# Two FFNs of an fp32 block: weight splits one unit further ahead, five plain pairs instead of six in the first

## The chip, the cores and the metric

The kernel runs on one core of a Trainium2 chip. The metric is the device time in microseconds (us) of one execution; 0.2% of it is 3.6 us.

## The reference, cut to what matters

One sequence of 512 tokens with 1024 features goes through an FFN, a mixer (short convolution and gated linear attention), a second FFN, and then a second block (neighbourhood attention, retention, a squared-ReLU MLP). All of it is float32. The change concerns the two FFNs, which are alike:

```python
def rmsnorm(x, g):
    xf = x.astype(jnp.float32)
    y = xf * lax.rsqrt(jnp.mean(xf * xf, axis=-1, keepdims=True) + EPS)
    return (y * g.astype(jnp.float32)).astype(x.dtype)

def swiglu(x, w_gu, w_down):          # w_gu: 1024 x 5632, w_down: 2816 x 1024
    g, u = jnp.split(x @ w_gu, 2, axis=-1)
    return (jax.nn.silu(g) * u) @ w_down

x = x + 0.5 * swiglu(rmsnorm(x, norm_ffn1_g[l]), ffn1_w_gu[l], ffn1_w_down[l])
x = x + hybrid_mixer(...)
x = x + 0.5 * swiglu(rmsnorm(x, norm_ffn2_g[l]), ffn2_w_gu[l], ffn2_w_down[l])
```

## The kernel before, in words

Activations lie transposed in SBUF: 8 tiles of 128 features x 512 tokens. TensorE multiplies in fp32r, so each fp32 operand is kept as a rounded high part and a low part that holds the rest, and a product is three matmuls: high x high, high x low, low x high.

**Units.** The whole program is a list of units (`_units`, line 81), numbered from 0, in the order in which TensorE takes them. A plain unit is one column tile of a weight matrix, 128 output features: 8 blocks x 3 matmuls of 512 columns (`unit`, line 1870; matmuls on L1884 to L1886). The weights of a unit are loaded by SyncE into `raw`, rounded by ScalarE into `wh` (`hi`, L526) and split by VectorE into `wl` (`lo`, L1065), which TensorE waits for. `raw`, `wh` and `wl` are rings of three plain units: ScalarE can round the weights of a unit only when TensorE is through with the unit three before it (`WF`, line 525).

**Pairs.** An FFN has 22 gate/up pairs (in groups of 8, 8 and 6, `FG`) and after each group 8 down units (`w_d`). The first `JS[f]` pairs of FFN f are plain: a gate unit and an up unit, 48 matmuls of 512 columns. The others are factored pairs (`pair`, line 1939): the 2x2 blocks of the two units are computed by seven products in place of eight, 7 x 4 x 3 = 84 matmuls of 256 columns. They need other operands:

- sums of weight blocks: `total` (VectorE, L1088), each then rounded (`pair_hi`, L536) and split (`pair_lo`, L1072) in half units of 512 columns;
- sums of activation blocks, built once per FFN for four values of `kp` by three steps on VectorE and one on ScalarE: `normed` (L1114, two instructions, needs the norm factor R), `sums_of_blocks` (four on L1119 to L1124), `operands` (ScalarE rounds them into BThi, L561), `low_blocks` (VectorE, the low part BTlo, L1128). TensorE starts the first factored pair when the fourth `low_blocks` is done (line 1944).

Between the products of a pair ScalarE copies partial results out of PSUM (`tap`, L552), and the third product waits for the first such copy (line 1950).

**What a plain pair j does on VectorE** (`ffn`, line 1202): the gate half times R (`times_r`, L1192), `low_blocks` of the previous pair's operands, silu times R (L1208), the product with the up half (L1249), the splits of two coming weight units, one step of the operands, and the low part of the result (`a_lo`, L1200). ScalarE does the silu (L588), two roundings, the high part of the result (L615) and `operands`.

**The order** is written out by hand for each engine, in two loops that mirror one another (`ffn` of ScalarE at line 585 and of VectorE at line 1202); each engine works through its own list in order. In the first FFN the norm factor is known only when units 0 to 2 are through: `norm` (line 577 and line 1168) takes one table load and three instructions on ScalarE (L571 to L575) between VectorE's L1160 and L1164. With `JS = (6, 5)` the first FFN has six plain pairs (units 0 to 11), and the operands are built from its third pair on (`normed(0, 0)` at the end of the second); the second FFN has five, and builds from its first.

Of the kernel before, what the change touches and what calls it, by code (L numbers as in the profile page):

```python
# [7 lines left out]
ALU = mybir.AluOpType  # L8
# [11 lines left out]
FT = FF // P  # L20
# [37 lines left out]
        self.eng.wait_ge(self.sem, self.n)  # L58


JS = (6, 5)
NP = 7

UNITS = []
# [214 lines left out]
def build(nc, dr, out):  # L279
# [20 lines left out]
    R, _ = sb("R", [P, T])  # L300
    SS, _ = sb("SS", [P, T])
    SS2, _ = sb("SS2", [P, T])
# [109 lines left out]
    def layer(u):  # L412
        return (u >= U0["ffn2"]) + (u >= U0["mlp"])

    def sums_of(p):
        return SS[:, :], SS2[:, :], TA[8], (TA[6], TA[7], SW3[:, :])[layer(p)]

    def part(p, c):

# [96 lines left out]
    def act_program(act):  # L516
# [60 lines left out]
        def norm(c):  # L577
            act.preload_act_table_set(LN_SET)
            rows(c, TA[6], TA[7], TA[8])
# [5 lines left out]
        def ffn(f, after):  # L585
# [8 lines left out]
            for g, (a, b) in enumerate(FG):  # L594
                for j in range(a, min(b, JS[f])):
                    u = GU[f, g] + 2 * (j - a)
                    if f == 0 and j == 0:
                        hi(3)
                        hi(4)
                        norm(1)  # L600
                    elif f == 0 and j == 1:
                        hi(5)
                    elif not JS[f] - 5 < j:
                        feed(u + 2)
                    if f == 1 and j == 0:
                        norm(6)
                    silu(u, j)
                    if f == 0 and j == 1:
                        hi(6)
                    elif f == 1 or j > 1:  # L610
                        feed(u + 3)
                    if f == 0 and j == 2:
                        operands(0, 0)
                    act.wait_ge(s["ev"], EVN[u + 1])
                    act.activation(Ahi[:, j - a, :], TA[6 + j % 2], ACT.Copy).then_inc(s["ah"], 1)  # L615
                    if JS[f] - 5 <= j < JS[f] - 1 and (f == 1 or j > 1):
                        feed(u + 4)
                        operands(f, j - JS[f] + 5)
                first = max(a, JS[f])
                for j in range(first, b):  # L620
                    p, v = GU[f, g] + 2 * (j - a), GU[f, g] + 2 * (j - a) + 2
# [428 lines left out]
    def dve_program(dve):  # L1050
# [114 lines left out]
            own.wait()  # L1165
            return lambda dst: dve.scalar_tensor_tensor(out=dst, in0=m, scalar=1.5, in1=y, op0=ALU.add, op1=ALU.mult)

        def norm(c, r):
            mean(c, TA[6], D)
            newton(c, TA[6], TA[7], TA[8])(R[:, :]).then_inc(s["r"], 1)  # L1170
            dve.wait_ge(s["r"], r)

# [27 lines left out]
            dve.tensor_tensor(Alo[:, j, :], src, f32(Ahi[:, j, :]), ALU.subtract).then_inc(s["al"], 1)  # L1200

        def ffn(f, after, sums):
            def gate(u, j):
                times_r(u, TA[j % 2])
                if JS[f] - 5 < j and (f == 1 or j > 2):
                    low_blocks(f, j - JS[f] + 4)
                dve.wait_ge(s["silu"], f * FT + j + 1)
                own.add(dve.tensor_tensor(TA[4 + j % 2], TA[2 + j % 2], R[:, :], ALU.mult))  # L1208

            def product(p, j):  # L1210
                dve.wait_ge(s["silu"], f * FT + j + 1)
                dve.wait_ge(s["ev"], EV0[p] + 2)
# [5 lines left out]
            for g, (a, b) in enumerate(FG):  # L1218
                for j in range(a, min(b, JS[f])):
                    u = GU[f, g] + 2 * (j - a)  # L1220
                    if f == 0 and j == 0:
                        lo(3)
                        lo(4)
                        norm(1, 1)
                    elif f == 0 and j == 1:
                        lo(5)
                    elif f == 0 and j == 2:
                        sums_of_blocks(0, 0)
                    elif j == JS[f] - 1:
                        total(u + 2, 0)  # L1230
                        total(u + 2, 1)
                        pair_lo(u + 2, 0)
                        pair_lo(u + 2, 1)
                    else:
                        feed(u + 2)
                    if f == 1 and j == 0:
                        norm(6, 3)
                    gate(u, j)
                    if f == 0 and j == 1:
                        lo(6)  # L1240
                    elif j < JS[f] - 1 and (f == 1 or j > 1):
                        feed(u + 3)
                    if f == 0 and j == 2:
                        low_blocks(0, 0)
                    if JS[f] - 5 <= j < JS[f] - 1 and (f == 1 or j > 1):
                        normed(f, j - JS[f] + 5)
                    dve.wait_ge(s["pe"], PEN[u + 1])
                    own.wait()
                    dve.tensor_tensor(TA[6 + j % 2], BK[BANK[u + 1]][:, :], TA[4 + j % 2],  # L1249
                                      ALU.mult).then_inc(s["ev"], 1)  # L1250
                    if f == 0 and j == 1:
                        normed(0, 0)
                    if JS[f] - 5 <= j < JS[f] - 1 and (f == 1 or j > 1):
                        sums_of_blocks(f, j - JS[f] + 5)
                    if j == JS[f] - 1:
                        pair_lo(u + 2, 2)
                        total(u + 2, 2)
                        pair_lo(u + 2, 3)
                    dve.wait_ge(s["ev"], EVN[u + 1])
                    a_lo(38 * f + a, j - a, TA[6 + j % 2])  # L1260
                    if j == JS[f] - 1:
                        total(u + 2, 3)
# [1269 lines left out]
```

## Time and profile before

| | |
|---|---|
| median of 3 runs | 1792.57 us (1792.3 to 1792.79) |
| profiled execution, its own time | 1793.07 us |
| its span | 1791.4 us |
| TensorE busy | 1780.2 us, 99% of the span, 9984 matmuls |
| VectorE busy | 1184.3 us, 66% |
| ScalarE busy | 801.1 us, 45% |
| DMA | 176.53 MB, mean 99 GB/s |

The median is 0.50 us under the profiled execution's own time. "Busy" counts an engine's instructions from their first start to their last end; matmuls are pipelined, so the length of one matters less than the distance from one start to the next. A wait is shown in square brackets before the instruction that had to wait, with the instruction that ended it.

### The profile page before, as it was taken

The numbers are of one execution on the slowest core, as the hardware profiler recorded it, in microseconds if no ns is written. First come the engines' busy times: TensorE is split into PE (matmuls) and PEld (weight loads), VectorE is DVE, ScalarE is ACT, GpSimd is POOL, SyncE is SP. The second block draws the span as 40 slices with busy tenths as digits, with TensorE's granted clock in tenths as the row PEclk, the third lists the DMA queues.
The fourth block names the chain that finished last, engine by engine and source line by source line (L and its number), as shares of the span: only waits on it lengthen the run. The fifth ranks groups of instructions, "written<-read, shape, count | busy, mean of one in ns | idle before, by whom it ended". The sixth has DMA issues, their size and how long they took to land.

```text
span 1791.4 us, 25308 instructions
## 1 busy us (share of the span) xinstructions
PE 1780.2 (99%) x9984; PEld 1542.5 (86%) x9984; DVE 1184.3 (66%) x1820; ACT 801.1 (45%) x1322; POOL 38.2 (2%) x38
## 2 busy tenths in 40 slices
PE   9999999999999999999999999999999999999998
PEld 7889989878888888888888998998877788989897
DVE  7948849647765534545695794876687677748474
ACT  6425525444332223423443462554655443627273
POOL 0000000000000000000000000000123000000000
PEclk9999999999999999999999999999999999999999
DMA  4232323332132332333324233233421233233232
GB/s 167 85 116 95 118 83 104 105 116 86 48 94 94 102 98 89 99 95 96 93 84 123 88 107 106 95 106 122 144 72 60 73 93 105 90 99 114 87 118 71
DMA packets 65252, 176.53 MB, mean 99 GB/s; under 512 B 7760, under 2 KB 9040, under 8 KB 65136
## 3 DMA queue, kind: packets, MB, share of 16 engines
q1 hardware_dynamic: 63408, 171.60, 30.9%
q10 hardware_dynamic: 1280, 2.08, 0.3%
q8 instruction: 80, 1.31, 0.3%
q0 software_dynamic: 448, 1.24, 0.3%
q14 instruction: 36, 0.29, 0.1%
HBM read 170.70 MB, written 2.10 MB: 96 GB/s over the span
## 4 chain that ended last, share of the span: by engine, by line
PE 96%; DVE 2%; ACT 1%; issue 1%; DMA 0%; DVEq 0%; ACTq 0%; POOLq 0%
PE ps L1884 20%; PE ps L1885 20%; PE ps L1886 20%; PE ps L1958 8%; PE ps L1961 8%; PE ps L1960 8%; PE ps L1906 2%; PE ps L1908 2%; PE ps L1907 2%; PE ps L2236 0%; PE ps L2247 0%; PE ps L2261 0%; PE ps L2108 0%; PE ps L1916 0%; PE ps L2111 0%
## 5 line engine op out<-in xcount | busy, mean ns | idle before, releaser
L1958 PE MATMUL ps<-BThi,wh 128*128 128x256 f32 x1260 | 353.5, 281 | 0.9 <-ACT tm L552 0.7
L1961 PE MATMUL ps<-BThi,wl 128*128 128x256 f32 x1260 | 351.7, 279 | 0.0
L1960 PE MATMUL ps<-BTlo,wh 128*128 128x256 f32 x1260 | 351.6, 279 | 0.0
L526 ACT ACTIVATE wh<-raw 128x1024 fp32r<-128x1024 f32 (+1 forms) x228 | 236.4, 1038 | 239.3 <-PE ps L1886 202.6
L1065 DVE TENSOR_TENSOR wl<-raw,wh 128x1024 fp32r<-128x1024 f32 (+1 forms) x228 | 275.8, 1210 | 101.7 <-ACT wh L526 100.0
L1884 PE MATMUL ps<-Hhi,wh 128*128 128x512 f32 x800 | 319.9, 400 | 1.8 <-DVE wl L1065 1.8
L1885 PE MATMUL ps<-Hlo,wh 128*128 128x512 f32 x800 | 312.4, 391 | 0.0
L1886 PE MATMUL ps<-Hhi,wl 128*128 128x512 f32 x800 | 312.2, 390 | 0.0
L1884 PE MATMUL ps<-Ahi,wh 128*128 128x512 f32 x792 | 308.5, 390 | 0.9 <-DVE Alo L1683 0.6
L1886 PE MATMUL ps<-Ahi,wl 128*128 128x512 f32 x792 | 308.2, 389 | 0.0
L1885 PE MATMUL ps<-Alo,wh 128*128 128x512 f32 x792 | 308.1, 389 | 0.0
L1958 PEld LDWEIGHTS ps<-BThi,wh 128*128 128x128 f32 x1260 | 236.4, 188 | 2.3 <-issue 1.1
L1961 PEld LDWEIGHTS ps<-BThi,wl 128*128 128x128 f32 x1260 | 236.8, 188 | 0.0
L1960 PEld LDWEIGHTS ps<-BTlo,wh 128*128 128x128 f32 x1260 | 235.8, 187 | 0.3
L1884 PEld LDWEIGHTS ps<-Hhi,wh 128*128 128x128 f32 x800 | 150.4, 188 | 38.9 <-issue 5.1
L1885 PEld LDWEIGHTS ps<-Hlo,wh 128*128 128x128 f32 x800 | 150.6, 188 | 33.0 <-issue 2.6
L1886 PEld LDWEIGHTS ps<-Hhi,wl 128*128 128x128 f32 x800 | 150.6, 188 | 31.9
L1884 PEld LDWEIGHTS ps<-Ahi,wh 128*128 128x128 f32 x792 | 148.6, 188 | 32.3 <-DVE Alo L1683 1.0
L1886 PEld LDWEIGHTS ps<-Ahi,wl 128*128 128x128 f32 x792 | 148.6, 188 | 31.1
L1885 PEld LDWEIGHTS ps<-Alo,wh 128*128 128x128 f32 x792 | 148.7, 188 | 30.5
L536 ACT ACTIVATE wh<-raw 128x512 fp32r<-128x512 f32 x135 | 84.7, 627 | 53.7 <-PE ps L1886 30.6
L1192 DVE TENSOR_TENSOR tm<-ps,R 128x512 f32<-128x512 f32 x71 | 49.0, 690 | 82.4 <-PE ps L1886 82.3
(307 smaller groups left out, 2106.2 us busy)
## 6 DMA issues: line engine op xcount, KB each, us to landing
raw<-in_w_gu SPq DMA_DIRECT2D x132, 256.0 KB, 2.9
raw<-in_w_d SPq DMA_DIRECT2D x32, 512.0 KB, 3.5
raw<-in_w_dn SPq DMA_DIRECT2D x32, 512.0 KB, 3.8
raw<-in_w_up SPq DMA_DIRECT2D x48, 256.0 KB, 2.9
raw<-in_w_gu SPq DMA_DIRECT2D x20, 512.0 KB, 3.5
raw<-in_w_d SPq DMA_DIRECT2D x16, 384.0 KB, 3.1
raw<-in_w_v SPq DMA_DIRECT2D x8, 512.0 KB, 3.9
raw<-in_w_cc SPq DMA_DIRECT2D x8, 512.0 KB, 3.5
```

Source lines behind the costliest of these rows:

```text
L526: act.activation(WH[WS[u]][:, 0:n], RAW[RSL[u]][:, 0:n], ACT.Copy).then_inc(s["wh"], 1)
L536: act.activation(WHP[WS[p][c]], part(p, c), ACT.Copy).then_inc(s["wh"], 1)
L1065: dve.tensor_tensor(WL[WS[u]][:, 0:n], RAW[RSL[u]][:, 0:n], f32(WH[WS[u]][:, 0:n]), ALU.subtract).then_inc(s["wl"], 1)
L1192: dve.tensor_tensor(dst, BK[BANK[u]][:, :], R[:, :], ALU.mult).then_inc(s["ev"], 1)
L1884: pe.matmul(ps, wh[:, c], hi[:, k, :], start=(k == 0), stop=False)
L1885: pe.matmul(ps, wh[:, c], lo[:, k, :], start=False, stop=False)
L1886: last = pe.matmul(ps, wl[:, c], hi[:, k, :], start=False, stop=(k == nb - 1))
L1906: pe.matmul(ps, Hhi[:, k, tc], wh[:, c], start=(k == 0), stop=False)
L1907: pe.matmul(ps, Hlo[:, k, tc], wh[:, c], start=False, stop=False)
L1958: pe.matmul(ps, whi[:, w], BThi[:, c, kp, :], start=(new and kp == 0), stop=False, skip_group_check=not new)
L1960: pe.matmul(ps, whi[:, w], BTlo[:, c, kp, :], start=False, stop=False, skip_group_check=not new)
L1961: last = pe.matmul(ps, wlo[:, w], BThi[:, c, kp, :], start=False, stop=(kp == 3), skip_group_check=not new)
```

## The change

`JS` becomes (5, 5): pair 5 of the first FFN (units 10 and 11) is factored instead of plain. In both FFNs the splits of the plain pairs are moved: before, pair j split the weights of units u+2 and u+3 (u its own gate unit), the first of them before `times_r`; now it splits u+3 and u+4, between `silu`, the product and the sums of blocks. The norm's part takes in one more rounding and split (unit 5 in the first FFN, u+3 in the second). The operands of the first FFN are built from pair 0 on, one `kp` in each of pairs 0 to 3. In the last plain pair, `total(…, 1)` comes after the silu product instead of before `times_r`.

```diff
-JS = (6, 5)
+JS = (5, 5)
...
     def sums_of(p):
-        return SS[:, :], SS2[:, :], TA[8], (TA[6], TA[7], SW3[:, :])[layer(p)]
+        return SS[:, :], SS2[:, :], TA[8], (TA[6 + JS[0] % 2], TA[6 + JS[1] % 2], SW3[:, :])[layer(p)]
...
             for g, (a, b) in enumerate(FG):
                 for j in range(a, min(b, JS[f])):
                     u = GU[f, g] + 2 * (j - a)
+                    kp = j - JS[f] + 5
                     if f == 0 and j == 0:
                         hi(3)
                         hi(4)
+                        hi(5)
                         norm(1)
-                    elif f == 0 and j == 1:
-                        hi(5)
-                    elif not JS[f] - 5 < j:
-                        feed(u + 2)
-                    if f == 1 and j == 0:
+                    elif j == 0:
+                        hi(u + 2)
+                        hi(u + 3)
                         norm(6)
                     silu(u, j)
-                    if f == 0 and j == 1:
-                        hi(6)
-                    elif f == 1 or j > 1:
-                        feed(u + 3)
-                    if f == 0 and j == 2:
-                        operands(0, 0)
+                    if f == 0 and j < 3:
+                        hi(6 + j)
+                    elif j == JS[f] - 1:
+                        pair_hi(u + 2, 2)
+                        pair_hi(u + 2, 3)
+                    elif j == JS[f] - 2:
+                        pair_hi(u + 4, 0)
+                        pair_hi(u + 4, 1)
+                    else:
+                        hi(u + 4)
                     act.wait_ge(s["ev"], EVN[u + 1])
                     act.activation(Ahi[:, j - a, :], TA[6 + j % 2], ACT.Copy).then_inc(s["ah"], 1)
-                    if JS[f] - 5 <= j < JS[f] - 1 and (f == 1 or j > 1):
-                        feed(u + 4)
-                        operands(f, j - JS[f] + 5)
+                    if 0 <= kp < 4:
+                        operands(f, kp)
+                    if j < JS[f] - 2 and (f == 1 or j > 1):
+                        hi(u + 5)
...
-        def norm(c, r):
+        def norm(c, r, u=None):
             mean(c, TA[6], D)
+            if u is not None:
+                lo(u)
             newton(c, TA[6], TA[7], TA[8])(R[:, :]).then_inc(s["r"], 1)
...
             for g, (a, b) in enumerate(FG):
                 for j in range(a, min(b, JS[f])):
                     u = GU[f, g] + 2 * (j - a)
+                    kp = j - JS[f] + 5
                     if f == 0 and j == 0:
                         lo(3)
                         lo(4)
-                        norm(1, 1)
...
+                        norm(1, 1, 5)
+                    elif j == 0:
+                        lo(u + 2)
+                        norm(6, 3, u + 3)
+                    times_r(u, TA[j % 2])
+                    if kp > 0:
+                        low_blocks(f, kp - 1)
+                    elif kp == 0:
+                        normed(f, kp)
+                    dve.wait_ge(s["silu"], f * FT + j + 1)
+                    own.add(dve.tensor_tensor(TA[4 + j % 2], TA[2 + j % 2], R[:, :], ALU.mult))
+                    if j == JS[f] - 1:
                         total(u + 2, 1)
...
+                    elif j > 0 and (f == 1 or j > 2):
+                        lo(u + 3)
+                    if j == JS[f] - 2:
+                        total(u + 4, 0)
+                    if 0 < kp < 4:
+                        normed(f, kp)
                     dve.wait_ge(s["pe"], PEN[u + 1])
                     own.wait()
                     dve.tensor_tensor(TA[6 + j % 2], BK[BANK[u + 1]][:, :], TA[4 + j % 2],
                                       ALU.mult).then_inc(s["ev"], 1)
...
+                    if f == 0 and j < 3:
+                        lo(6 + j)
+                    elif j < JS[f] - 2:
+                        lo(u + 4)
+                    elif j == JS[f] - 2:
+                        pair_lo(u + 4, 0)
+                        pair_lo(u + 4, 1)
+                    else:
                         pair_lo(u + 2, 2)
                         total(u + 2, 2)
                         pair_lo(u + 2, 3)
+                    if 0 <= kp < 4:
+                        sums_of_blocks(f, kp)
                     dve.wait_ge(s["ev"], EVN[u + 1])
                     a_lo(38 * f + a, j - a, TA[6 + j % 2])
```

How the instructions stand, at three places. **ScalarE, first FFN, around the norm** (L526 rounds a weight unit, L578 is the norm's table load, L571 its first instruction; - is before, + is the change):

```order
 L567 ACTIVATE tm_60<-X 128x512
 L567 ACTIVATE tm_61<-X 128x512
-L526 ACTIVATE wh<-raw 128x1024 x2
+L526 ACTIVATE wh<-raw 128x1024 x3
 L578 ACT_TABLE_LOAD
 L571 ACTIVATE tm_67<-tm_66 128x512
```

A third rounding, that of unit 5, now stands ahead of the norm's table load. It used to stand behind the first pair's high part.

**VectorE, first FFN, one plain pair before** (pair 3; from `times_r` to the split of unit 10, the next pair's first):

```order
L1192 TENSOR_TENSOR tm_61<-ps,R 128x512
L1128 TENSOR_TENSOR BTlo<-BF,BThi 128x7x256
L1208 TENSOR_TENSOR tm_65<-tm_63,R 128x512
L1065 TENSOR_TENSOR wl<-raw,wh 128x1024
L1114 SCALAR_TENSOR_TENSOR BF<-X,vec,R 128x2x256 x2
L1249 TENSOR_TENSOR tm_67<-ps,tm_65 128x512
L1119 TENSOR_TENSOR BF<-BF 128x256
L1120 TENSOR_TENSOR BF<-BF 128x256
L1122 TENSOR_TENSOR BF<-BF 128x256
L1124 TENSOR_TENSOR BF<-BF 128x256
L1200 TENSOR_TENSOR Alo<-tm_67,Ahi 128x512
L1065 TENSOR_TENSOR wl<-raw,wh 128x1024
```

and the same place with the change (pair 2, which builds the same `kp` + 1; its lines are 7 further on: L1199 is `times_r`, L1133 `low_blocks`, L1235 silu times R, L1119 `normed`, L1246 the product, L1070 a split, L1124 to L1129 the sums, L1207 `a_lo`):

```order
L1199 TENSOR_TENSOR tm_60<-ps,R 128x512
L1133 TENSOR_TENSOR BTlo<-BF,BThi 128x7x256
L1235 TENSOR_TENSOR tm_64<-tm_62,R 128x512
L1119 SCALAR_TENSOR_TENSOR BF<-X,vec,R 128x2x256 x2
L1246 TENSOR_TENSOR tm_66<-ps,tm_64 128x512
L1070 TENSOR_TENSOR wl<-raw,wh 128x1024
L1124 TENSOR_TENSOR BF<-BF 128x256
L1125 TENSOR_TENSOR BF<-BF 128x256
L1127 TENSOR_TENSOR BF<-BF 128x256
L1129 TENSOR_TENSOR BF<-BF 128x256
L1207 TENSOR_TENSOR Alo<-tm_66,Ahi 128x512
```

One split has left each of pairs 1 and 2, and the split that stays (of unit 8 in pair 2) stands behind the product.

**VectorE, first FFN, the last but one plain pair with the change** (pair 3, up to the two half splits of the first factored pair; L1093 is `total`, L1077 `pair_lo`):

```order
L1199 TENSOR_TENSOR tm_61<-ps,R 128x512
L1133 TENSOR_TENSOR BTlo<-BF,BThi 128x7x256
L1235 TENSOR_TENSOR tm_65<-tm_63,R 128x512
L1070 TENSOR_TENSOR wl<-raw,wh 128x1024
L1093 TENSOR_TENSOR SS<-raw 128x512
L1119 SCALAR_TENSOR_TENSOR BF<-X,vec,R 128x2x256 x2
L1246 TENSOR_TENSOR tm_67<-ps,tm_65 128x512
L1077 TENSOR_TENSOR wl<-raw,wh 128x512
L1077 TENSOR_TENSOR wl<-SS,wh 128x512
```

The split of unit 9 stands behind `low_blocks` and the silu product; `total` and the two half splits, which stood in the last plain pair ahead of its `times_r`, have come into this one.

## Rows read from the trace of the kernel before

**Rows 1.** Page, part 1: busy time and share of each engine.

```profile
PE 1780.2 (99%) x9984; PEld 1542.5 (86%) x9984; DVE 1184.3 (66%) x1820; ACT 801.1 (45%) x1322; POOL 38.2 (2%) x38
```

**Rows 2.** Waits of PE: who for whom, us in total, times, longest.

```profile
PE ps L1884 <- DVE wl L1065: 1.8, 1, 1.8
```

**Rows 3.** Timeline of PE, first FFN: start us, length us, instruction, [wait before].

```profile
17.71 0.39 PE L1886 MATMUL ps<-Hhi,wl 128*128 128x512 f32 x1
...
22.47 0.39 PE L1886 MATMUL ps<-Hhi,wl 128*128 128x512 f32 x1
...
50.57 0.39 PE L1886 MATMUL ps<-Hhi,wl 128*128 128x512 f32 x1
52.78 0.50 PE L1884 MATMUL ps<-Hhi,wh 128*128 128x512 f32 x1 [1.82 <-DVE wl L1065]
...
76.32 0.30 PE L1958 MATMUL ps<-BThi,wh 128*128 128x256 f32 x1
...
79.04 0.28 PE L1961 MATMUL ps<-BThi,wl 128*128 128x256 f32 x1
79.85 0.36 PE L1958 MATMUL ps<-BThi,wh 128*128 128x256 f32 x1 [0.53 <-ACT tm L552]
...
97.28 0.39 PE L1884 MATMUL ps<-Ahi,wh 128*128 128x512 f32 x1
```

**Rows 4.** Windows: stretch, us, PE, PEld, DVE, ACT, POOL busy, PEclk, DMA share, GB/s.

```profile
54.00:58.00 4.00, 4.00 (x12) 3.10 (x12) 4.00 (x5) 0.94 (x1) 0.00 (x0) 0.57 0.38 133
```

**Rows 5.** Timeline of DVE, first FFN: plain pair 3.

```profile
52.64 0.68 DVE L1192 TENSOR_TENSOR tm<-ps,R 128x512 f32<-128x512 f32 x1
53.24 2.02 DVE L1128 TENSOR_TENSOR BTlo<-BF,BThi 128x1792 fp32r<-128x1792 f32 x1
55.18 0.68 DVE L1208 TENSOR_TENSOR tm<-tm,R 128x512 f32<-128x512 f32 x1
55.78 1.22 DVE L1065 TENSOR_TENSOR wl<-raw,wh 128x1024 fp32r<-128x1024 f32 x1
56.91 1.41 DVE L1114 SCALAR_TENSOR_TENSOR BF<-X,vec,R 128x512 f32<-128x512 f32 x2
58.43 0.69 DVE L1249 TENSOR_TENSOR tm<-ps,tm 128x512 f32<-128x512 f32 x1
59.04 0.42 DVE L1119 TENSOR_TENSOR BF<-BF 128x256 f32<-128x256 f32 x1
...
60.63 0.69 DVE L1200 TENSOR_TENSOR Alo<-tm,Ahi 128x512 fp32r<-128x512 f32 x1
61.23 1.22 DVE L1065 TENSOR_TENSOR wl<-raw,wh 128x1024 fp32r<-128x1024 f32 x1
```

**Rows 6.** Timeline of ACT, first FFN: norm, operands, first copy out of PSUM.

```profile
24.48 0.64 ACT L571 ACTIVATE tm<-tm 128x512 f32<-128x512 f32 x1 [1.36 <-DVE tm L1160]
...
60.74 1.71 ACT L561 ACTIVATE BThi<-BF 128x1792 fp32r<-128x1792 f32 x1
...
79.34 0.36 ACT L552 ACTIVATE tm<-ps 128x256 f32<-128x256 f32 x1
```

**Rows 7.** Timeline of ACT, second block: a table load and its successor.

```profile
1243.33 1.28 ACT L803 ACT_TABLE_LOAD   x1
1244.63 0.22 ACT L804 ACTIVATE small<-vec 128x16 f32<-128x16 f32 x1
```

**Rows 8.** Timeline of DVE, first FFN: plain pair 0.

```profile
27.93 0.69 DVE L1192 TENSOR_TENSOR tm<-ps,R 128x512 f32<-128x512 f32 x1
29.32 0.69 DVE L1208 TENSOR_TENSOR tm<-tm,R 128x512 f32<-128x512 f32 x1 [0.70 <-ACT tm L588]
30.12 0.69 DVE L1249 TENSOR_TENSOR tm<-ps,tm 128x512 f32<-128x512 f32 x1
```

**Rows 9.** Timeline of DVE, second FFN: the last low part of the operands.

```profile
923.60 2.02 DVE L1128 TENSOR_TENSOR BTlo<-BF,BThi 128x1792 fp32r<-128x1792 f32 x1
```

**Rows 10.** Timeline of PE, second FFN: start of the first factored pair.

```profile
927.90 0.28 PE L1958 MATMUL ps<-BThi,wh 128*128 128x256 f32 x1
```

More of the change, by code:

```diff
@@ L1202, in ffn @@
         def ffn(f, after, sums):
[L1203 to L1208, printed above, removed]
             def product(p, j):
@@ L1223, in ffn @@
                         lo(4)
-                        norm(1, 1)
[L1225 to L1230, printed above, removed]
-                        total(u + 2, 1)
[L1232 to L1246, printed above, removed]
+                        norm(1, 1, 5)
[10 more added lines that the diff above has]
+                    if j == JS[f] - 1:
+                        total(u + 2, 1)
+                    elif j > 0 and (f == 1 or j > 2):
[4 more added lines that the diff above has]
+                        normed(f, kp)
                     dve.wait_ge(s["pe"], PEN[u + 1])
@@ L1250, in ffn @@
                                       ALU.mult).then_inc(s["ev"], 1)
[L1251 to L1255, printed above, removed]
+                    if f == 0 and j < 3:
[6 more added lines that the diff above has]
+                    else:
                         pair_lo(u + 2, 2)
```

## The prediction

> **What bounds the kernel now.** I read the page's busy times first. TensorE is busy for 99% of the span, VectorE for 66% [rows 1]: only fewer or faster matmuls, or fewer stalls of TensorE, can shorten the run. The waits of PE come next: the longest is one of 1.8 us, for a weight split [rows 2]. The timeline of PE puts it at the start of unit 8, plain pair 4 of the first FFN, at 52.78 [rows 3]. Right behind it, from 54 to 58, the mean granted clock is 0.57 [rows 4], so most of that stretch ran at 1.2 GHz and not at 2.4. Between 17.71 and 22.47 lie 21 starts: 0.227 us per matmul of 512 columns, 5.44 us per plain unit, 10.88 per plain pair [rows 3]. Units 8 to 11 should take 21.76 us; they take 23.54 (52.78 to 76.32), so the slow clock cost 1.8 us on top of the stall. Between 76.32 and 79.04 lie 23 starts of 256 columns: 0.118 us each, 9.9 us for the 84 of a factored pair. The two such pairs of that group end at 97.28, after 20.96 us, 1.2 more than 2 x 9.9; the largest part is the wait at 79.85 [rows 3].
>
> Everything that the change can reach lies before 97.28, and in the same stretch of the second FFN. So I lay out where the first down unit starts (97.28 before).
>
> **The matmuls.** One plain pair becomes factored: 10.88 - 9.9 = 1.0 us less. If no stall came, and the old one with its slow clock went too, another 2.0 + 1.8 us would go.
>
> **VectorE's chain, first FFN.** The first factored pair waits for four low parts, and their building now begins at the norm factor. TensorE without stalls would reach that pair (unit 10 now) at 50.80 + 2 x 5.44 = 61.7, 50.80 being where the stalled unit 8 was due (50.57 + 0.23) [rows 3]. When is VectorE there? I take distances from start to start in plain pair 3 [rows 5]:
> - `times_r` 0.60, low part 1.94, silu product 0.60, split 1.13, `normed` 1.52, product 0.61, four sums 1.59, `a_lo` 0.60. In this pair VectorE does not pause.
> - A wait that pair 3 before hid: ScalarE rounds the sums from 60.74 for 1.71 [rows 6], i.e. it ends 3.41 after the first sum's start (59.04). Before, a split, `a_lo` and `times_r` lay between. Now only `a_lo` and `times_r` do, and VectorE is back at the low part 1.59 + 0.60 + 0.60 = 2.79 after the first sum: it waits about 0.65 us, four times.
>
> The start also moves. Unit 5's rounding now stands ahead of the norm's table load, and it needs unit 2's place in `wh`, which TensorE leaves with the matmul at 22.47 [rows 3]; with its length of 0.39 and 0.1 that I allow for the release (an estimate) the rounding starts at 22.96. By its size it takes 0.98 or a little more (1.71 x 1024 / 1792 [rows 6]), so it ends at 24.0, and the table load of 1.28 [rows 7] at 25.3. The norm's first instruction stood at 24.48 [rows 6]: it comes 0.83 us later, and `times_r` of pair 0 at 27.93 + 0.83 = 28.76 [rows 8].
>
> Then, pair by pair (starts of `times_r`):
> - Pair 0: 0.60 + `normed` 1.32 (nothing behind it depends on it) + silu product to product 0.80 [rows 8] + 0.60 + split 1.13 + 1.59 + 0.60 = 6.64, to 35.40.
> - Pairs 1 and 2: 0.60 + 0.65 + 1.94 + 0.60 + 1.52 + 0.61 + 1.13 + 1.59 + 0.60 = 9.24 each, to 44.64 and 53.88.
> - Pair 3 has a `total` (0.60) and two half splits (1.20) more: 11.04, to 64.92.
> - Pair 4: 0.60 + 0.65 + 2.02: the fourth low part is done at 68.19.
>
> **What TensorE sees.** Unit 8's split ends at 44.64 + 5.92 + 1.22 = 51.78, due 50.80: a stall of 1.0, where it was 2.0. Unit 9's split stands behind a low part and ends at 53.88 + 3.79 + 1.22 = 58.89, due 57.25: 1.7 more. The factored pair is due at 64.4 and starts at 68.2: 3.8 more. If the clock falls behind the first two stalls, that is hidden under the third, which VectorE ends. VectorE's lateness is thus 6.5 us in all: the splits come earlier, but the operands do not come early enough for one plain pair fewer.
>
> **The first factored pair.** Its third product waits for a ScalarE copy that stands behind the rounding of the third weight sum. Before, with VectorE ahead, it waited for the copy at 79.34 and started at 79.85, 3.53 after the pair began [rows 3, 6]. Now the silu product, `total(1)`, the product, a half split (0.6 each, the split 0.1 late) and the third sum come after the fourth low part, then rounding and copy: about 4.15 after the pair began. I take 4.3, since the clock may still be slow there. Five products of 1.41 and 0.1 of small waits follow: the pair ends at 79.65. Two more pairs, 19.8, with 0.4 of waits as the pairs before had: the first down unit starts at 99.85 or so. **That is 2.6 us later than 97.28.**
>
> **Second FFN.** It had five plain pairs already, and TensorE sets the pace: the last low part ends at 925.62 and the factored pair starts at 927.90 [rows 9, 10], 2.28 to spare. The delay of the norm by some 0.8 is taken up before that, and later splits have a unit's length of cover. I cost it at nothing. If that cover were gone the price would be that of the first pair's waits, up to 1.2 us; the gain can be as much if the third product's wait shrinks. DMA: the transfers are the same bytes; those for units 7 to 9 now wait for splits that come at or before their old times, and a plain unit's transfer has more than 5 us to land. Nothing.
>
> **Sum.** -1.0 (matmuls) - 3.8 (old stall and slow clock) + 6.5 (three new stalls) + about 0.9 (waits inside the factored pairs: 2.1 in three where two had 1.2) = +2.6 us. On the profiled execution's 1793.07 that is 1795.7; its own time is 0.50 above the median of 1792.57, so the median comes to **1795.2 us**, 0.15% longer. About 0.2% (3.6 us) is what a measurement here can tell from no change, so the forecast is "within".
>
> **A page against a row.** After a table load, the next ScalarE instruction starts 0.01 us behind its end (1244.63 after 1243.33 + 1.28) [rows 7], so my 0.83 holds no further cost. The Trainium skill, ScalarE: Activation LUTs, section "What ACT_TABLE_LOAD costs", adds a drain of about 1.38 us to every switch of table; the trace does not show it here. By that page the norm, and with it VectorE's whole chain, would be a further 1.4 us late, and the sum +4.0.
>
> **Rivals.**
> 1. *The slow clock outlasts the third stall* (17%). One wait of 1.82 us was enough for a clock of 0.57 over 4 us [rows 3, 4], and now 3.8 us of idleness stand right before the factored pair. The least it can cost is what I took, 0.15; the most is a second time the 1.8 that it cost before. I take 1.2: +3.8, 1796.4, slower. It decides if the clock stays at 1.2 GHz for more than some 2.5 us after the pair starts. Against it: the tap's wait of 1.3 us absorbs part.
> 2. *The whole gain comes* (4%). VectorE's waits shrink so that the fourth low part is done by 61.7; all three stalls go: -1.0 - 3.8 + 0 + 0.4 = -4.4, 1788.2. It decides from a low part done before 65.6 for any gain at all. Against it: the instructions alone from 28.76, without one wait, take 36.8 us, to 65.6, so my durations would have to be wrong too.
> 3. *Null* (12%). Waits for ScalarE's rounding do not come (4 x 0.65 = 2.6 us less): +0, 1792.6. For it: only that no such round trip is exposed before by more than 0.4 us. Against it: the order gives VectorE nothing else to do.
> 4. *The table load drains* (5%): +4.0, 1796.6. The row speaks against it.
> 5. *A new wait in the second FFN* (6%): there too unit u+3 is rounded ahead of the norm's table load. If it costs TensorE 1.2 us: +3.8, 1796.4.
> 6. *The order is not what the change says*: no; the order of the instructions shows splits and operands moved as described, in both FFNs.
>
> **How the numbers follow.** My forecast has 56%. Slower by over 0.2%: rivals 1, 4 and most of 5, 27% with a little from the forecast's own spread. Faster: rival 2, 4%. Within: 69%. The forecast's own range is 1794.2 to 1796.2 (0.1 us per round trip, 0.5 for the clock). Reaching to the null at the lower end and to rival 1 with the full 1.8 and some of rival 5 at the upper one, the range is 1792.3 to 1797.4; the whole gain is left out.
>
> **What would show it.** Starts of PE: unit 8 at 51.8 after a wait of 1.0, unit 9 at 58.9 or later, the factored pair at 68.2 after an idle stretch of 2 to 3.8 us ended by the low part (L1133), the down units at 99.9. VectorE: `times_r` at 28.8, 35.4, 44.6, 53.9 and 64.9, with a wait of 0.65 for ScalarE's BThi before each low part. ScalarE: the norm's first instruction at 25.3. Second FFN: its factored pair starts as long after its first unit as before. A factored pair that starts before 65.6, or no waits for BThi, would prove the chain wrong.

## The result, and the profile after

The changed kernel took **1796.07 us** (median of 16 runs, 1795.37 to 1797.04) against 1792.30 for the kernel before (16 runs beside it): ratio 1.0021, 95% interval 1.0014 to 1.0028, that is 3.8 us longer. Measured again (`after_again` below) it was 1796.51 against 1792.82, ratio 1.0021 (1.0012 to 1.0030). The forecast was 1795.2, range 1792.3 to 1797.4; 1796.07 lies in the range, 0.9 us above the forecast. The profiled execution took 1795.58, of which 1793.4 are the span; before it was 1793.07 and 1791.4.

The page of the changed kernel, part 1, answers to [rows 1]: TensorE is busy for 3.6 us less, yet the span is 2.0 longer.

```profile
PE 1776.6 (99%) x10020; PEld 1540.4 (86%) x10020; DVE 1187.9 (66%) x1831; ACT 803.2 (45%) x1330; POOL 38.2 (2%) x38
```

Where the time is lost stands in the timeline of PE, first FFN (start us, length us, instruction, [wait before]), which answers to [rows 3]:

```profile
51.80 0.50 PE L1886 MATMUL ps<-Hhi,wh 128*128 128x512 f32 x1 [0.89 <-DVE wl L1070]
58.92 0.50 PE L1886 MATMUL ps<-Hhi,wh 128*128 128x512 f32 x1 [1.35 <-DVE wl L1070]
68.22 0.39 PE L1960 MATMUL ps<-BThi,wh 128*128 128x256 f32 x1 [3.56 <-DVE BTlo L1133]
72.44 0.36 PE L1960 MATMUL ps<-BThi,wh 128*128 128x256 f32 x1 [1.13 <-ACT tm L552]
75.56 0.36 PE L1960 MATMUL ps<-BThi,wh 128*128 128x256 f32 x1 [0.16 <-ACT tm L552]
...
99.59 0.40 PE L1886 MATMUL ps<-Ahi,wh 128*128 128x512 f32 x1
```

The one wait of 1.82 us before has become three: a split at unit 8, a split at unit 9, and the fourth low part of the operands at the first factored pair. The down units start at 99.59, where it was 97.28: 2.3 us later. Behind that the two programs run alike. The first factored pair of the second FFN starts 2.37 us later than in [rows 10]:

```profile
930.27 0.28 PE L1960 MATMUL ps<-BThi,wh 128*128 128x256 f32 x1
```

VectorE's timeline shows why the third wait comes. These are the first `times_r`, then `times_r` and low part of pairs 1 and 4 (the chain of [rows 5, 8], with its new waits):

```profile
28.73 0.69 DVE L1199 TENSOR_TENSOR tm<-ps,R 128x512 f32<-128x512 f32 x1
...
35.38 0.68 DVE L1199 TENSOR_TENSOR tm<-ps,R 128x512 f32<-128x512 f32 x1
36.63 2.02 DVE L1133 TENSOR_TENSOR BTlo<-BF,BThi 128x1792 fp32r<-128x1792 f32 x1 [0.57 <-ACT BThi L561]
...
64.90 0.68 DVE L1199 TENSOR_TENSOR tm<-ps,R 128x512 f32<-128x512 f32 x1
66.14 2.02 DVE L1133 TENSOR_TENSOR BTlo<-BF,BThi 128x1792 fp32r<-128x1792 f32 x1 [0.56 <-ACT BThi L561]
```

And ScalarE, at the start of the norm (answers to [rows 6, 7]): unit 5's rounding, the table load behind it, and the norm's first instruction 0.80 us later than before.

```profile
22.91 1.06 ACT L526 ACTIVATE wh<-raw 128x1024 fp32r<-128x1024 f32 x1 [0.74 <-PE ps L1888]
23.98 1.28 ACT L578 ACT_TABLE_LOAD   x1
25.28 0.64 ACT L571 ACTIVATE tm<-tm 128x512 f32<-128x512 f32 x1
```

### The profile page after: what moved, and what is told of

It reads as the page before. It is cut to its first block, busy times and chain, and to the rows that moved or that the text cites. A ratio compares the mean times of both kernels' runs of the same rounds, so it can differ in the third digit from the quotient of the medians.

```text
span 1793.4 us, 25415 instructions
## 1 busy us (share of the span) xinstructions
PE 1776.6 (99%) x10020; PEld 1540.4 (86%) x10020; DVE 1187.9 (66%) x1831; ACT 803.2 (45%) x1330; POOL 38.2 (2%) x38
## 3 DMA queue, kind: packets, MB, share of 16 engines
q0 software_dynamic: 448, 1.24, 0.2%
## 4 chain that ended last, share of the span: by engine, by line
PE 95%; DVE 3%; ACT 1%; issue 1%; DMA 0%; DVEq 0%; ACTq 0%; POOLq 0%
PE ps L1886 20%; PE ps L1887 20%; PE ps L1888 20%; PE ps L1960 8%; PE ps L1963 8%; PE ps L1962 8%; PE ps L1908 2%; PE ps L1910 2%; PE ps L1909 2%; PE ps L2238 0%; PE ps L2249 0%; DVE wl L1070 0%; PE ps L2263 0%; PE ps L2110 0%; ACT BThi L561 0%
## 5 line engine op out<-in xcount | busy, mean ns | idle before, releaser
L1960 PE MATMUL ps<-BThi,wh 128*128 128x256 f32 x1288 | 361.2, 280 | 5.5 <-DVE BTlo L1133 3.6
L1963 PE MATMUL ps<-BThi,wl 128*128 128x256 f32 x1288 | 359.0, 279 | 0.0
L1962 PE MATMUL ps<-BTlo,wh 128*128 128x256 f32 x1288 | 358.9, 279 | 0.0
L526 ACT ACTIVATE wh<-raw 128x1024 fp32r<-128x1024 f32 (+1 forms) x226 | 234.1, 1037 | 248.2 <-PE ps L1888 209.9
L1070 DVE TENSOR_TENSOR wl<-raw,wh 128x1024 fp32r<-128x1024 f32 (+1 forms) x226 | 273.2, 1210 | 102.5 <-ACT wh L526 100.7
L1886 PE MATMUL ps<-Hhi,wh 128*128 128x512 f32 x784 | 313.1, 399 | 2.2 <-DVE wl L1070 2.2
L1887 PE MATMUL ps<-Hlo,wh 128*128 128x512 f32 x784 | 305.5, 390 | 0.0
L1888 PE MATMUL ps<-Hhi,wl 128*128 128x512 f32 x784 | 305.5, 390 | 0.0
L1960 PEld LDWEIGHTS ps<-BThi,wh 128*128 128x128 f32 x1288 | 241.7, 188 | 7.8 <-DVE BTlo L1133 4.0
L1963 PEld LDWEIGHTS ps<-BThi,wl 128*128 128x128 f32 x1288 | 242.1, 188 | 0.0
L1962 PEld LDWEIGHTS ps<-BTlo,wh 128*128 128x128 f32 x1288 | 241.0, 187 | 0.3
L1199 DVE TENSOR_TENSOR tm<-ps,R 128x512 f32<-128x512 f32 x70 | 48.3, 690 | 83.0 <-PE ps L1888 82.8
```

What stands on the lines that cost most here:

```text
L526: act.activation(WH[WS[u]][:, 0:n], RAW[RSL[u]][:, 0:n], ACT.Copy).then_inc(s["wh"], 1)
L1070: dve.tensor_tensor(WL[WS[u]][:, 0:n], RAW[RSL[u]][:, 0:n], f32(WH[WS[u]][:, 0:n]), ALU.subtract).then_inc(s["wl"], 1)
L1199: dve.tensor_tensor(dst, BK[BANK[u]][:, :], R[:, :], ALU.mult).then_inc(s["ev"], 1)
L1886: pe.matmul(ps, wh[:, c], hi[:, k, :], start=(k == 0), stop=False)
L1887: pe.matmul(ps, wh[:, c], lo[:, k, :], start=False, stop=False)
L1888: last = pe.matmul(ps, wl[:, c], hi[:, k, :], start=False, stop=(k == nb - 1))
```

## The experiments

Two theories were to be told apart. **The chain:** the operands of the factored pairs are one chain on VectorE without slack, so every microsecond of it shows at the factored pair, and five plain pairs give it too little time. **The rival:** something else holds TensorE (the second FFN, a transfer, the clock), or VectorE's work costs whatever its place. "Start" below is the start of the first factored pair; "first down" that of the first down unit.

| kernel | median, us | before beside it | ratio (95%) | start | first down |
|---|---|---|---|---|---|
| after_again | 1796.51 | 1792.82 | 1.0021 (1.0012-1.0030) | 68.26 | 100.10 |
| e1_six_plain | 1791.07 | 1792.82 | 0.9990 (0.9981-0.9999) | 73.68 | 95.33 |
| e2_splits_in_wait | 1795.55 | 1792.82 | 1.0014 (1.0005-1.0024) | 66.92 | 99.65 |
| e3_table_first | 1795.76 | 1792.82 | 1.0016 (1.0007-1.0025) | 67.54 | 99.38 |
| e4_pad_in_wait | 1796.61 | 1792.88 | 1.0022 (1.0013-1.0031) | 68.57 | 99.89 |
| e5_pad_behind | 1798.05 | 1792.88 | 1.0029 (1.0017-1.0040) | 70.28 | 102.14 |
| e6_second_only | 1792.92 | 1792.88 | 1.0000 (0.9992-1.0009) | 76.27 | 97.05 |
| e8_six_table_splits | 1792.47 | 1792.88 | 0.9999 (0.9990-1.0007) | 74.91 | 96.56 |
| e7_six_table_first | 1790.24 | 1792.61 | 0.9988 (0.9979-0.9997) | 73.47 | 94.85 |
| e9_six_highs_too | 1788.71 | 1792.61 | 0.9979 (0.9970-0.9987) | 72.42 | 93.34 |
| e10_five_six | 1796.26 | 1792.61 | 1.0019 (1.0010-1.0029) | 67.90 | 100.50 |

Whole timelines differ by some tenths of a microsecond in their origin from one execution to the next, so small differences are read as distances within a profile.

### The changed kernel again

> The changed kernel once more, for its clock and as the reference on this chip. Theory (VectorE's chain from the norm factor sets the start of the first factored pair): the same starts as in its first profile: factored pair 68.2, first down unit 99.6, within 0.1 where the clock stays at 2.4 GHz. Second part of the theory, on the 1.2 us by which the median of 16 runs is slower than the profile's difference: in some executions the clock falls behind the waits of unit 8, unit 9 or the pair; then the first down unit starts up to 1.8 later (101.4). Rival: the median is slower for another reason, and the profile shows a later first down unit with the clock at 1.00 throughout.

The 3.7 us came back. Its profile caught another state of the clock. The windows behind the factored pair's start, first of the changed kernel's first profile (stretch, us, busy PE, PEld, DVE, ACT, POOL, PEclk, DMA share, GB/s):

```profile
68.00:70.00 2.00, 1.78 (x15) 1.78 (x16) 1.97 (x4) 0.60 (x2) 0.00 (x0) 1.00 0.00 0
70.00:72.00 2.00, 1.31 (x12) 1.11 (x10) 1.93 (x4) 1.69 (x5) 0.00 (x0) 1.00 0.00 0
72.00:74.00 2.00, 1.56 (x14) 1.59 (x15) 1.90 (x4) 1.10 (x4) 0.00 (x0) 1.00 0.42 118
```

and of this one, where the two products of the pair run at half the clock and the wait of 1.13 us before the third is used up by it:

```profile
68.00:70.00 2.00, 1.74 (x13) 1.74 (x14) 2.00 (x4) 0.56 (x2) 0.00 (x0) 0.89 0.00 0
70.00:72.00 2.00, 2.00 (x11) 2.00 (x11) 1.90 (x5) 1.68 (x5) 0.00 (x0) 0.50 0.00 0
72.00:74.00 2.00, 2.00 (x15) 1.99 (x15) 1.90 (x4) 1.09 (x4) 0.00 (x0) 0.76 0.41 108
```

The first down instruction stands at 100.10 here for 99.59. This was the usual case: of the seven profiles below and above with five plain pairs in the first FFN, six show a stretch at half the clock at or behind the pair's wait, all but the changed kernel's first. From the pair's start to the first down unit, 31.37 us without it, they take 31.84 here and 32.60 in e10, whose first FFN is the same, so the stretch cost 0.5 and 1.2 us; the variants lie between 31.32 (e4) and 32.73 (e2).

For executions without a trace there is only the mean granted clock over the span, and it is a rough sign: in ten of the thirteen profiles the clock is also below 1.00 in the last 4 us (e6's has 0.65 there, a mean of 0.999 and no slow stretch at unit 8). Of the first 16 runs of the changed kernel two have 1.000 (spans 1793.2 and 1793.4), five 0.999 (median span 1793.5) and nine 0.998 (median 1794.3), 1.0 us apart; of the 11 runs here one has 1.000 (1794.1), three 0.999 (1794.1) and seven 0.998 (1794.7), 0.6 apart. In the kernel before the mean makes no difference: of the 33 runs in this comparison 22 have 0.999 (median span 1791.2) and eleven 1.000 (1791.3).

### Six plain pairs in the new order

```diff
-JS = (5, 5)
+JS = (6, 5)
```

> JS = (6, 5) again, everything else as in the change: new order of splits, but six plain pairs and the operands one pair later. Theory: VectorE's chain gives the fourth low part at 73.8 (28.73 + 4.53 for pair 0 without normed and sums + 6.6 + 9.2 + 10.4 + 11.0 + 3.2), the pair is due at 72.6, so one wait of about 1.3 us and none at units 8 to 11; first down unit at 95.2, 2.1 before the kernel before's 97.28 and 4.4 before the change's. Time 1.0 to 2.2 us under the kernel before. Rival (the new order itself costs, through the waits for ScalarE's BThi): first down unit at 97.3 or later, time as before or slower.

This one line makes 1791.07, 5.4 us under the changed kernel and 1.75 under before. The waits at units 8 and 9 are gone; what is left on PE is the wait for the low part and the one for the copy:

```profile
73.68 0.39 PE L1960 MATMUL ps<-BThi,wh 128*128 128x256 f32 x1 [1.23 <-DVE BTlo L1133]
77.91 0.36 PE L1960 MATMUL ps<-BThi,wh 128*128 128x256 f32 x1 [1.13 <-ACT tm L552]
```

So the new order gains, and taking a plain pair away loses more than that: with the pair left in, VectorE's chain has 10.9 us more until it is needed.

### Splits in the idle 0.57 us

The low parts of units 8 and 9 (and the second `total` before the pair) move on VectorE from behind the silu product to just ahead of the low blocks, with ScalarE's high parts moved to match:

```diff
+                    if f == 0 and j in (2, 3):
+                        lo(6 + j)
+                    if f == 0 and j == 4:
+                        total(u + 2, 1)
                     if kp > 0:
                         low_blocks(f, kp - 1)
```

> Five plain pairs. In pairs 2 and 3 of the first FFN the splits of units 8 and 9 stand between times_r and the low part, in VectorE's wait for BThi, and in pair 4 total(1) does; ScalarE rounds units 8 and 9 one step earlier. Theory (only the end of VectorE's chain counts): three waits of 0.57 go, the fourth low part ends at 66.5 where it was 68.2, units 8 and 9 do not wait at all, and the pair starts at 66.5 after a wait of 4.8 us: first down unit at 97.9, 1.7 before the change's 99.6. Rival (the three waits of TensorE add up to the loss): taking away the first two (2.6 us by excess) gives 2.6 or more, first down unit at 97.0 or earlier.

The stalls of units 8 and 9 went, and the pair started 1.34 us earlier than in `after_again`. The forecast was 1.7, from three waits of 0.57. Only two of them shortened the chain: the `total` of the last pair had stood behind the fourth low part, so in that pair it only filled the wait (the low part starts 1.24 after `times_r`, as before the move). TensorE had idled longer in one piece, though:

```profile
66.92 0.58 PE L1969 MATMUL ps<-BThi,wh 128*128 128x256 f32 x1 [5.10 <-DVE BTlo L1136]
```

Behind it the clock is 0.50 up to 72, and all 11 runs have 0.998. Of the 1.34 us only 0.45 were left at the first down unit (99.65), in the median 0.96. The forecast for that unit, 97.9, was missed by 1.75 us, and the rival's 97.0 by more: the theory had the start nearly right and no term for the slow clock behind it.

### Table load first

```diff
-                        hi(5)
-                        norm(1)
+                        norm(1, 5)
```

where `norm(c, u)` loads the table, then rounds unit u's high part, then starts on the norm.

> Five plain pairs. Only unit 5's rounding moves: behind the norm's table load instead of ahead of it, so the table load fills ScalarE's idle time. Theory: norm's first instruction at 24.5 where it was 25.28, times_r of pair 0 at 27.95, everything on VectorE 0.8 earlier: pair starts at 67.4, first down unit at 98.8, time 0.8 under the change. Rival (VectorE waits elsewhere and swallows it): no difference to the change, 99.6.

The pair came 0.72 us earlier with the same wait before it (3.56), the first down unit 0.72 earlier, the median 0.75. The load's place is 0.7 of the 0.8 us that the prediction counted for it.

### One instruction more, ahead of the low part or behind it

```diff
+                    if f == 0 and 0 < j < 4:
+                        own.add(dve.tensor_tensor(SS2[:, :], R[:, :], R[:, :], ALU.mult))
                     if kp > 0:
                         low_blocks(f, kp - 1)
```

> The changed kernel with one more VectorE instruction of 128 x 512 values (0.6 us, into a tile that nothing reads before it is written again) in pairs 1 to 3 of the first FFN, right ahead of the low part, where the changed kernel idles 0.57 us for ScalarE's BThi. Theory (the low part ends by ScalarE's BThi, so what is put ahead of it costs only what exceeds the idle 0.57 us): the three idle stretches vanish, the first factored pair starts 0.1 us later (68.3 after 68.2), first down instruction at 99.7, median within 0.3 us of the changed kernel's. Rival (VectorE's work counts whole wherever it stands): each adds 0.6 us, the pair starts at 70.0, the median rises by 1.8.

> The same three instructions, but right behind the low part, where VectorE does not idle. Theory (VectorE's chain is without slack from the first pair to the first factored pair, apart from the waits for BThi): each counts whole, the first factored pair starts 1.8 us later, at 70.0, after a wait of 5.4, and the first down instruction stands 1.8 to 2.5 us later (the more if the clock falls behind the longer wait); median 1.8 to 2.5 over the changed kernel's. Rival (the wait at the factored pair is set by something else, a transfer or ScalarE): starts unmoved, median unmoved.

Ahead of the low part, the instruction fills the idle time. VectorE in pair 1:

```profile
35.71 0.68 DVE L1199 TENSOR_TENSOR tm<-ps,R 128x512 f32<-128x512 f32 x1
36.31 0.68 DVE L1231 TENSOR_TENSOR SS<-R 128x512 f32<-128x512 f32 x1
36.96 2.03 DVE L1133 TENSOR_TENSOR BTlo<-BF,BThi 128x1792 fp32r<-128x1792 f32 x1
```

The low part starts 1.25 us after `times_r`, exactly as without the extra instruction (36.63 - 35.38). The whole timeline stands 0.3 us later from `times_r` on, and so does the pair (68.57 for 68.26): the three cost nothing, and the median rose by 3.73 over before's, where the changed kernel's rose by 3.69. Behind the low part, the same three cost all they take:

```profile
35.62 0.68 DVE L1199 TENSOR_TENSOR tm<-ps,R 128x512 f32<-128x512 f32 x1
36.88 2.02 DVE L1133 TENSOR_TENSOR BTlo<-BF,BThi 128x1792 fp32r<-128x1792 f32 x1 [0.57 <-ACT BThi L561]
38.82 0.69 DVE L1235 TENSOR_TENSOR SS<-R 128x512 f32<-128x512 f32 x1
```

The pair starts at 70.28, 1.7 later than with the instruction ahead, and the median is 1.44 more. This is the cleanest sign for the chain. One part of my expectation was wrong: the wait before the pair stays 3.55 and does not grow to 5.4, because all three instructions stand ahead of unit 9's split. Unit 9 itself starts 1.71 later (60.98 for 59.27), as much as the pair does; the wait that grows is the one at unit 8, from 0.91 to 2.11.

### The new order in the second FFN alone

The loops take the old body where `f == 0` and the new one where `f == 1`.

> The second FFN in the change's order, the first FFN in the order of before with its six plain pairs. Theory (the second FFN's new order neither gains nor costs, as the two traces' equal stretches from its first factored pair on say): first down instruction of the first FFN at 97.3, first factored pair of the second at 927.9, median that of before within 0.3. Rival (part of the 3.8 us lies behind the first FFN): median 0.5 to 1.5 over before.

1792.92 against 1792.88; the second FFN's pair starts at 927.72, in before's profile at 927.90, 830.67 and 830.62 us behind the first down unit: the second FFN neither gains nor loses. This profile holds a surprise about the first FFN, where the kernel is the old one. Its stall at unit 8 was followed by no slow clock (windows as above; [rows 4] has 0.57 here):

```profile
54.00:58.00 4.00, 4.00 (x20) 3.27 (x19) 4.00 (x5) 1.00 (x2) 0.00 (x0) 1.00 0.37 125
```

and still the factored pair starts at the same time as in [rows 3] (76.32), after a wait:

```profile
76.27 0.39 PE L2035 MATMUL ps<-BThi,wh 128*128 128x256 f32 x1 [1.34 <-DVE BTlo L1157]
```

### Table load and splits, with six plain pairs

On the six-pair version: the table load first, and the low parts of units 9 and 11 ahead of the low blocks.

```diff
+                    if f == 0 and j in (3, 4):
+                        lo(u + 3)
                     if kp > 0:
                         low_blocks(f, kp - 1)
```

> The new order with six plain pairs in the first FFN, with the table load ahead of unit 5's high part on ScalarE (0.8 us earlier VectorE chain), and the low parts of units 9 and 11 on VectorE moved to just ahead of the low blocks, into the idle 0.57 us for BThi (1.1 us). Theory (the 1.39 us in front of the first factored pair of the six-pair version is VectorE's chain alone): the chain is 1.9 us earlier, the wait goes, the pair starts at 72.3 to 72.5, first down instruction at 94.0 to 94.3, median 1789.7 (1.3 under the six-pair version's, 3.1 under before's). Rival (the next things on the way come late instead: a split for units 8 to 11, or ScalarE's parts behind the pair's start): waits of up to 1.3 us elsewhere, median 1791.

A miss: 1792.47, slower than the six-pair version. I had read VectorE's queue and not ScalarE's. ScalarE makes these high parts behind BThi, so VectorE waited for them at the head of its queue. In pair 3, on VectorE:

```profile
50.45 1.22 DVE L1071 TENSOR_TENSOR wl<-raw,wh 128x1024 fp32r<-128x1024 f32 x1 [1.51 <-ACT wh L526]
51.59 2.02 DVE L1134 TENSOR_TENSOR BTlo<-BF,BThi 128x1792 fp32r<-128x1792 f32 x1
```

First the table load was then tried without the splits:

> The new order with six plain pairs in the first FFN and the table load ahead of unit 5's high part on ScalarE, nothing else. In the version before it (e8) ScalarE's high parts of units 9 and 11 stood behind BThi, so the low parts that were moved ahead of the low blocks waited 1.51 us each, and took the 0.8 us of the table load and more. Theory (without the two moves the 0.8 us stay): first factored pair at 72.9, after a wait of 0.5 to 0.7 in place of 1.39, first down instruction at 94.5, median 0.8 under the six-pair version's, 1.9 to 2.6 under before's, about 1790.3. Rival (something else than VectorE's chain holds the pair, so that e8's loss came from elsewhere): pair at 73.7, median as the six-pair version's.

The wait before the pair fell from 1.23 to 0.45 us, that is by the 0.8 forecast, and the median to 2.4 under before's, 0.6 further than the six-pair version was under its own. The start itself, 73.47, is only 0.2 earlier and misses the forecast 72.9: in this execution TensorE reaches the pair at 73.02, where it was there at 72.45.

Then e8 again, with ScalarE's high parts moved too:

```diff
+                    if f == 0 and j in (2, 3):
+                        hi(u + 5)
                     if 0 <= kp < 4:
                         operands(f, kp)
-                    if j < JS[f] - 2 and (f == 1 or j > 1):
+                    if j < JS[f] - 2 and f == 1:
                         hi(u + 5)
```

> As e8, with ScalarE's high parts of units 9 and 11 moved ahead of its BThi as well, into its idle 2.1 us there. Theory (e8's 1.51 us waits were these high parts alone): the two waits are gone and VectorE's chain is 1.9 us ahead of the six-pair version's, the first factored pair starts when units 2 to 11 end, at 72.3, third product's wait at 76.5 as before (1.3) or less, first down instruction at 94.0, median 1789.7. Rival (unit 9's and 11's high parts now delay BThi, or wait for their slots): waits of up to 1 us at BThi, pair at 73, median 1790.5 to 1791.

**1788.71 us**, 3.9 under before (ratio 0.9979, 0.9970 to 0.9987) and 7.4 to 7.8 under the changed kernel's two medians: the version that beats both. VectorE no longer waits in pair 3, and TensorE not at the pair:

```profile
48.27 0.68 DVE L1202 TENSOR_TENSOR tm<-ps,R 128x512 f32<-128x512 f32 x1
48.87 1.21 DVE L1073 TENSOR_TENSOR wl<-raw,wh 128x1024 fp32r<-128x1024 f32 x1
50.00 2.02 DVE L1136 TENSOR_TENSOR BTlo<-BF,BThi 128x1792 fp32r<-128x1792 f32 x1
```

```profile
72.42 0.28 PE L1965 MATMUL ps<-BThi,wh 128*128 128x256 f32 x1
...
75.92 0.36 PE L1965 MATMUL ps<-BThi,wh 128*128 128x256 f32 x1 [0.51 <-ACT tm L552]
```

It did 1.0 better than forecast; a part of that is the third product's wait, which shrank as well (0.51 for 1.13).

### Five plain pairs, then six

```diff
-JS = (5, 5)
+JS = (5, 6)
```

> The changed kernel with six plain pairs in the second FFN in place of five, so that the whole program has as many instructions as before's, with the first FFN as changed. It is for the time that lies outside the span (2.2 us in the changed kernel's executions, 1.6 in before's and in the six-pair version's). Theory A (it goes with the size of the program): 1.6 outside. Theory B (it goes with the first FFN's five pairs): 2.2 outside. Inside the span: first FFN as changed (first down instruction at 99.6 to 100.1); the second FFN has 10.9 for 9.9 us at one pair, so the span is 1.0 us longer, unless splits come late there.

The median is 3.65 over before's, as the changed kernel's. The median span is 3.7 over before's (1794.65 for 1790.95), where the changed kernel's was 3.1 over: 0.6 more, of the 1.0 forecast. The first down unit came 0.4 after the stretch I had given, with the clock at 1.2 GHz from within the pair's wait up to 73.5. The time outside the span (an execution's own time less its span, median over the runs) is 1.63 here, like the 1.61 to 1.63 of before and of every kernel with six and five pairs, while the kernels with five and five (the changed one, e2, e3) have 2.17 to 2.20. So it does not go with the first FFN's five pairs. That it goes with the size alone is not shown: e4 and e5 are larger by three instructions and have 2.03 and 1.91, on another chip, on which the changed kernel itself was not run.

## Why the prediction was nearly right

**VectorE's chain.** Forecast `times_r` at 28.76, 35.40, 44.64, 53.88 and 64.92; measured 28.73, 35.38, 44.61, 53.85 and 64.90. Waits for BThi: forecast 0.65, four times; measured 0.57. The chain could be laid out because every length was in [rows 5, 8] and the only new thing was one wait, taken from two starts. The same chain moved by what e3, e4 and e5 put into it.

**What TensorE sees.** Units 8 and 9 at 51.8 and 58.9 and the pair at 68.2: measured 51.80, 58.92 and 68.22. The third product came 4.22 after the pair's start (forecast 4.3), the first down unit at 99.59 (forecast 99.85, since less was lost inside the factored pairs than the 0.9 I added). So +2.3 where the sum had +2.6.

**The term "old stall and slow clock, -3.8"** was right as a distance and wrong as a cause. I wrote that the slow clock "cost 1.8 us on top of the stall". It did not: e6's execution, with the same first FFN and no slow clock, has a wait for the low part in its place. VectorE ended the stretch either way, at 76.3. Before's own trace shows it too: the fourth low part ends at 76.17, and the pair starts at 76.32 [rows 3].

```profile
74.15 2.02 DVE L1128 TENSOR_TENSOR BTlo<-BF,BThi 128x1792 fp32r<-128x1792 f32 x1
```

With VectorE's chain alone the sum reads more simply. From the pair's start to the first down unit, three factored pairs take 31.37 us (99.59 - 68.22) where two took 20.96 [rows 3], 10.4 more. So the start had to come 10.4 earlier to break even, and the fourth low part let it come 8.1 earlier (68.22 for 76.32): 2.3 later in all. The slow stretch was free because without it a wait of its length stood there.

**From the profile to the median.** Profile against profile the span grew by 2.0 us; the medians are 3.7 to 3.8 apart. Before's profiled execution (1793.07) was 0.77 us slower than the median beside the result, the changed kernel's 0.49 faster than its own, and the two are 2.51 apart, 0.5 of it outside the span. In the second comparison, 3.69 splits into 0.56 outside the span (2.17 for 1.61), a thing the prediction had no term for, and 3.1 of median span (1794.3 for 1791.2). Of that the undisturbed profile shows 2.0 to 2.3. The rest, 0.8 to 1.1, is of the size of **rival 1**: the clock falls at or behind the third stall in six of the seven profiles, and costs 0.5 and 1.2 in the two with the changed first FFN, where I took 1.2 and gave it 17%. That all of the rest is the clock is not shown: the one run of `after_again` with a mean clock of 1.000 has a span of 1794.1, 2.9 over before's median, and what lies behind the first down unit varies by 0.8 us between profiles (1693.6 to 1694.4). Rival 1 was the usual case and not the one in six: its 1796.4 is nearer to the measured 1796.07 than the forecast's 1795.2. Counted from before's median, the forecast had +2.6 and the measurement +3.8; the range held it because it reached up to rival 1, and the 0.56 outside the span had no term in either. The condition that I named (1.2 GHz for over 2.5 us after the pair starts) was met in `after_again`; the tap's wait absorbed a part, as I had held against it.

**The other rivals.** The whole gain (2) did not come: it would take a low part done 6.5 us earlier. The null (3) supposed no waits for BThi: they are there, four times. The table load (4) has no drain behind it: it ends at 25.26 and its successor starts at 25.28 (0.02 behind; the 0.01 that I read from [rows 7] is 0.02 as well). The Trainium skill, ScalarE: Activation LUTs, section "What ACT_TABLE_LOAD costs", adds about 1.38 us; the trace disagrees. A new wait in the second FFN (5) is ruled out by e6.

## What to carry to other kernels

When work is removed from the engine that bounds the kernel, ask first whether the next engine's chain fits into the time that is left: here one pair fewer took 10.9 us of cover from a chain that had none to spare, and the same reordering with the pair left in was faster than both. An idle piece of 0.6 us in front of a wait is free room for an instruction only if that instruction's own operand is already there, so two queues have to be moved together. In the kernel before, a slow-clock stretch cost nothing because a later wait swallowed it; with the change, a stretch behind the last wait cost 0.5 to 1.2 us.

## What the runs showed of the hardware

- After one and the same wait the clock may fall or not. The wait of some 1.8 us at unit 8 was followed by a granted clock of 0.57 in before's profile and of 1.00 in e6's; the wait of 3.56 at the factored pair by 1.00 in one execution of the changed kernel and 0.50 in another (from 69.5 to 73.0), and in e10's, with the same first FFN, the clock was at 0.50 from 66.8 to 73.5. After the longest wait, 5.10 us, the mean clock was 0.998 in all 11 runs. Two profiles of one kernel can thus differ by half a microsecond without a difference in the kernel.
- Some 0.56 us of difference lay outside the span, in a program of 25,415 instructions against 25,308. What it is stays open; e10 says only that it does not come with the first FFN's five pairs alone.
